# Last expert's down projection in two halves of its columns: the first half's rows put back and added before the second half is done

## The reference

```python
def swiglu(h, w_up, w_down):
    g, u = jnp.split(h @ w_up, 2, axis=-1)
    return (jax.nn.silu(g) * u) @ w_down

def moe_swiglu(h, w_router, w_up, w_down):
    logits = jnp.einsum('bld,de->ble', h, w_router, ...)
    top_v, top_i = lax.top_k(logits, TOP_K)          # TOP_K = 2
    top_w = jax.nn.softmax(top_v, axis=-1)
    combine = ...                                     # (tokens, 8), two entries per token
    out = jnp.zeros(h.shape, jnp.float32)
    for e in range(N_EXPERTS):                        # 8 experts
        out = out + combine[..., e:e + 1] * swiglu(h, w_up[e], w_down[e])
    return out.astype(h.dtype)

# x = x + moe_swiglu(rms_norm(x), ...);  y_prompt, y_sample are x after this layer
```

## Time and profile before

| | |
|---|---|
| median of 3 runs | 2094.9 us (2094.56 to 2096.92) |
| span of the profiled execution (first to last instruction) | 2093.1 us |
| PE busy | 2059.4 us (98%) |
| DVE, ACT, POOL busy | 788.0, 405.0, 157.3 us |
| DMA: bytes moved | 548.81 MB; about 410 GB/s over the experts |
| last expert's down projection, PE | 672 MATMULs, 2043.07 to 2084.1 us |
| from its end to the last instruction | 9.0 us |

### The profile page before, as it was taken

How to read it: one execution, slowest core, us unless ns; L and a number is a source line. 1 busy time by engine, 2 the same in 40 slices (tenths; PEclk the granted TensorE clock), 3 DMA queues, 4 the chain that set the end, 5 groups by cost and what they waited for, 6 DMA issues and landing times.

```text
span 2093.1 us, 45743 instructions
## 1 busy us (share of the span) xinstructions
PE 2059.4 (98%) x20245; PEld 1494.6 (71%) x20245; DVE 788.0 (38%) x1501; ACT 405.0 (19%) x772; POOL 157.3 (8%) x222
## 2 busy tenths in 40 slices
PE   7999999999999999999999999999999999999998
PEld 5977777778999997777777746565665656565645
DVE  5896333545676578643255310010101010101013
ACT  3423424312221143433341200000000000000000
POOL 3501020000000031112100010000000000000001
PEclk9999999999999999999999999999999999999999
DMA  5434535695554543453477699999999999999996
GB/s 168 142 109 142 171 115 162 190 276 155 149 154 147 159 141 122 128 161 116 151 202 229 258 364 412 408 411 409 411 409 411 408 410 410 405 415 396 412 410 241
DMA packets 287993, 548.81 MB, mean 262 GB/s; under 512 B 12883, under 2 KB 218501, under 8 KB 271348
## 3 DMA queue, kind: packets, MB, share of 16 engines
q1 hardware_dynamic: 279808, 535.85, 70.9%
q10 hardware_dynamic: 6644, 5.58, 0.9%
q0 software_dynamic: 1344, 4.45, 0.6%
HBM read 527.15 MB, written 22.50 MB: 263 GB/s over the span
## 4 chain that ended last, share of the span: by engine, by line
PE 96%; DVE 2%; POOL 1%; issue 1%; ACT 1%; POOLq 0%; DVEq 0%; ACTq 0%
PE bank L1080 93%; PE bank L1086 3%; ACT mem L2056 1%; DVE mem L2542 0%; DVE mem L2879 0%; DVE mem L2546 0%; DVE hflat L2575 0%; POOL quarterm L937 0%; DVE mem L2905 0%; POOL lmask L913 0%; POOL lmask L915 0%; DVE col L2912 0%; DVE hflat L2542 0%; DVE mem L2916 0%; DVE xT L3428 0%
## 5 line engine op out<-in xcount | busy, mean ns | idle before, releaser
L1080 PE MATMUL bank<-mem 128*32 128x256 f32 (+9 forms) x13288 | 1100.5, 387 | 11.3 <-DVE mem L2879 3.5
L1080 PEld LDWEIGHTS bank<-mem 128*32 128x32 f32 (+3 forms) x13288 | 793.8, 128 | 298.5 <-issue 47.7
L1080 PE MATMUL bank<-hflat,mem 128*128 128x288 f32 (+3 forms) x2688 | 572.8, 371 | 0.9 <-ACT hflat L2056 0.7
L1080 PEld LDWEIGHTS bank<-hflat,mem 128*128 128x128 f32 (+2 forms) x2688 | 443.3, 188 | 102.9 <-issue 12.2
L2056 ACT ACTIVATE mem<-bank 128x288 f32<-128x288 f32 (+10 forms) x423 | 180.1, 430 | 822.9 <-PE bank L1080 758.3
L1080 PE MATMUL bank<-mem,steps 128*32 128x384 f32 (+1 forms) x3072 | 290.8, 539 | 0.0
L1080 PEld LDWEIGHTS bank<-mem,steps 128*32 128x32 f32 x3072 | 148.2, 110 | 139.0 <-issue 24.7
L2542 DVE TENSOR_TENSOR mem<-mem 128x512 f32<-128x512 f32 (+10 forms) x336 | 234.6, 725 | 29.0 <-PE bank L1080 18.5
L2546 DVE SCALAR_TENSOR_TENSOR hflat<-hflat,bank 128x512 f32<-128x512 f32 x24 | 15.1, 683 | 410.8 <-ACT hflat L2056 410.8
L2056 ACT ACTIVATE hflat<-bank 128x512 f32<-128x512 f32 (+1 forms) x40 | 19.6, 554 | 567.4 <-PE bank L1080 567.4
L2056 ACT ACTIVATE mem<-mem 128x1152 f32<-128x1152 f32 (+9 forms) x125 | 92.1, 739 | 99.2 <-DVE mem L2634 63.9
(11 more groups left out here) (250 smaller groups left out, 740.4 us busy)
## 6 DMA issues: line engine op xcount, KB each, us to landing
mem<-in_w_moe_up_dram SPq DMA_DIRECT2D x64, 2048.0 KB, 20.9
mem<-in_w_moe_down_dram SPq DMA_DIRECT2D x56, 2048.0 KB, 21.3
mem<-in_w_moe_up_dram SPq DMA_DIRECT2D x32, 2304.0 KB, 22.9
mem<-in_w_in_dram SPq DMA_DIRECT2D x70, 1024.0 KB, 5.3
mem<-in_w_moe_up_dram SPq DMA_DIRECT2D x16, 1536.0 KB, 21.8
mem<-in_w_ffn_up_dram SPq DMA_DIRECT2D x44, 512.0 KB, 5.2
mem<-in_cache_kv_w_dram SPq DMA_DIRECT2D x26, 512.0 KB, 4.8
mem<-in_cache_kv_w_dram SPq DMA_DIRECT2D x74, 128.0 KB, 4.9
```

The source lines that it names most:

```text
L1080: return mm(out, lhsT, rhs, start=start, stop=stop, skip_group_check=True)
```

## The change

Only the last expert's down projection and what follows it are changed; the other experts run the same code, and their instructions keep their order.

- The 28 row blocks by 1024 columns are taken as two halves of 512 columns. Seven slabs still carry them (`last_down`): eight row blocks of half a width each, slab 17 (SHARED) with the last four of half 0 and the first four of half 1. A slab is still 2 MB, but in rows of 2048 bytes, and slab 17 comes in two DMAs.
- A product now has 128 columns in place of 256, so a slab has 96 products, which is 192 pairs of MATMUL and LDWEIGHTS. Half 0 accumulates in bank 6, half 1 in bank 7.
- ACT copies half 0 (128 x 384) when slab 17 has been used, half 1 (128 x 384) after slab 20.
- PE puts half 0 back, all three token blocks, between slab 18 and slab 19 (`rows_put_back(0, tb)`: 36 products of 128 columns, 72 pairs), into banks 0 to 3; half 1 behind slab 20, in the order of before (tb 0, tb 1, a wait for DVE's first addition of half 1, tb 2).
- DVE first waits for half 0's rows and adds them (three instructions over 512 columns), then the six additions of the gathered rows and the rank steps, then half 1 (three over 512 columns).
- SP stores six pieces of 512 columns in place of three of 1024: half 0's three when the gathered rows are in, half 1's as they are added.
- The wait for slab 17's weights counts two landings (`eslab_in`), and the counts of the semaphore `y_added` go from 9 to 12 in a round.

```diff
+        last_down = [((0, 0, 8),), ((0, 8, 8),), ((0, 16, 8),), ((0, 24, 4), (1, 0, 4)), ((1, 4, 8),), ((1, 12, 8),),
+                     ((1, 20, 8),)]
+        SHARED = 17
...
+                        if kind == "d" and e == NEXP - 1:
+                            c0 = 0
+                            for h, row, rows in last_down[n - 14]:
+                                sp.dma_start(eslot[n % MRING][:, c0:c0 + 512 * rows].rearrange("p (k n) -> p k n", k=rows),
+                                             down_v[:, e, row:row + rows, 512 * h:512 * h + 512]
+                                             ).then_inc(slab_here[n % MRING], 16)
...
+                for h in range(2):
+                    for b, (t0, n) in enumerate(BLK):
...
+                        sp.wait_ge(y_added, 12 * r + (9 if h == 0 else 10 + b))
+                        sp.dma_start(dst[:, 512 * h:512 * h + 512], xrow[b][0:n, 512 * h:512 * h + 512]
+                                     ).then_inc(out_stored, 16)
...
+                    def last_slab_down(n):
+                        pe.wait_ge(*eslab_in(r, e, n))
+                        c0 = 0
+                        for h, row, rows in last_down[n - 14]:
+                            w = eslot[n % MRING][:, c0:c0 + 512 * rows].rearrange("p (k n) -> p k n", k=rows)
+                            for i in range(rows):
+                                t = row + i
+                                for b in range(TT):
+                                    for o in range(4):
+                                        ins = put(bank[y_bank[h]][32 * o:32 * o + 32, P * b:P * b + P],
+                                                  hidT[:, b, t, :], w[:, i, P * o:P * o + P], t == 0 and b == 0, t == 27)
+                            c0 += 512 * rows
+                        ins.then_inc(*lup("m_slab"))
+
+                    def rows_put_back(h, tb):
+                        nt = BLK[tb][1]
+                        for b in range(TT):
+                            for o in range(4):
+                                rows = slice(32 * o, 32 * o + 32)
+                                acc = bank[o + (4 if h and tb == 1 else 0)][0:nt, P * tb:P * tb + P]
+                                ins = put(acc, last_cols[b][rows, BLK[tb][0]:BLK[tb][0] + nt],
+                                          yb[rows, b, P * h:P * h + P], b == 0 and (h == 1 or tb == 0), b == TT - 1)
+                        if h == 1 or tb == 2:
+                            ins.then_inc(last_rows, 1)
...
-                        if n == 17:
+                        if n == (17 if e < NEXP - 1 else 15):
                             pe.wait_ge(*lat("m_hidT", it, 2 * TT))
+                        if e == NEXP - 1 and n == SHARED + 1:
+                            pe.wait_ge(*lat("m_y", it, 1))
+                            for tb in range(3):
+                                rows_put_back(0, tb)
...
-                for tb, (t0, nt) in enumerate(BLK):
+                pe.wait_ge(y_added, 12 * r + 3)
+                pe.wait_ge(*lat("m_y", expert(r, NEXP - 1), 2))
+                for tb in range(3):
                     if tb == 2:
-                        pe.wait_ge(y_added, 9 * r + 7)
+                        pe.wait_ge(y_added, 12 * r + 10)
...
+                    rows_put_back(1, tb)
...
+                        for h in range(2):
+                            act.wait_ge(*lat("m_slab", it, done_after["d"] if h else SHARED + 1))
+                            fn(yb[:, :, P * h:P * h + P], bank[6 + h][:, 0:3 * P].rearrange("p (b n) -> p b n", b=TT),
+                               ACT.Copy).then_inc(*lup("m_y"))
...
+                def add_last(h, b):
+                    n = BLK[b][1]
+                    x = xrow[b][0:n, 512 * h:512 * h + 512].rearrange("t (o c) -> t o c", o=4)
+                    y0 = 4 if h and b == 1 else 0
+                    ve.scalar_tensor_tensor(x, banks[0:n, y0:y0 + 4, P * b:P * b + P], masked[0:n, b, 1:2], x,
+                                            ALU.mult, ALU.add).then_inc(y_added, 1)
+                dve.wait_ge(last_rows, 4 * r + 1)
+                for b in range(3):
+                    add_last(0, b)
                 dve.wait_ge(rows_back, 96 * (r + 1))
...
-                for b, (t0, n) in enumerate(BLK):
-                    dve.wait_ge(last_rows, 3 * r + b + 1)
-                    x = xrow[b][0:n, :].rearrange("t (o c) -> t o c", o=4)
...
+                for b in range(3):
+                    dve.wait_ge(last_rows, 4 * r + b + 2)
+                    add_last(1, b)
```

More of the change, by code:

```diff
@@ L700, in eslab_view, with eslab_in @@
             return eslot[n % MRING][:, 0:nk * w].rearrange("p (k n) -> p k n", k=nk)
-        def eslab_in(it, n):
-            return slab_here[n % MRING], 16 * (it * PERSLOT + n // MRING + 1)
+        def eslab_in(r, e, n):
+            count = 16 * (expert(r, e) * PERSLOT + n // MRING + 1)
+            if n % MRING == SHARED % MRING:
+                count = count + 16 * r + (16 if e == NEXP - 1 and n == SHARED else 0)
+            return slab_here[n % MRING], count
         def eslab_used(it, n):
@@ L873, in _ @@
                         load_rounds(sp, end)
-                for b, (t0, n) in enumerate(BLK):
-                    dst = y_prompt[0, t0:t0 + n, :] if t0 < TP else y_sample.rearrange("b i d -> (b i) d")
-                    sp.wait_ge(y_added, 9 * r + 7 + b)
-                    sp.dma_start(dst, xrow[b][0:n, :]).then_inc(out_stored, 16)
+                for h in range(2):
+                    for b, (t0, n) in enumerate(BLK):
+                        dst = y_prompt[0, t0:t0 + n, :] if t0 < TP else y_sample.rearrange("b i d -> (b i) d")
+                        sp.wait_ge(y_added, 12 * r + (9 if h == 0 else 10 + b))
+                        sp.dma_start(dst[:, 512 * h:512 * h + 512], xrow[b][0:n, 512 * h:512 * h + 512]
+                                     ).then_inc(out_stored, 16)
             sp.wait_ge(stored, 16 * stores[0])
@@ L1972, in slab_down @@
                         c = eslabs[n][1] // 4
-                        pe.wait_ge(*eslab_in(it, n))
+                        pe.wait_ge(*eslab_in(r, e, n))
                         w = eslab_view(n)
@@ L2012, in _ @@
                     for n in range(14, 21):
-                        slab_down(n)
-                        if n == 17:
+                        if e < NEXP - 1:
+                            slab_down(n)
+                        else:
+                            last_slab_down(n)
+                        if n == (17 if e < NEXP - 1 else 15):
                             pe.wait_ge(*lat("m_hidT", it, 2 * TT))
+                        if e == NEXP - 1 and n == SHARED + 1:
+                            pe.wait_ge(*lat("m_y", it, 1))
+                            for tb in range(3):
+                                rows_put_back(0, tb)
                     if e == 0:
                         load_rounds(pe, end)
-                for tb, (t0, nt) in enumerate(BLK):
+                pe.wait_ge(y_added, 12 * r + 3)
+                pe.sem_inc(wait_passed, 1)
+                pe.wait_ge(*lat("m_y", expert(r, NEXP - 1), 2))
+                pe.sem_inc(wait_passed, 1)
+                for tb in range(3):
                     if tb == 2:
-                        pe.wait_ge(y_added, 9 * r + 7)
+                        pe.wait_ge(y_added, 12 * r + 10)
                         pe.sem_inc(wait_passed, 1)
[L2022 to L2030, removed]
+                    rows_put_back(1, tb)
+                pe.wait_ge(y_added, 12 * r + 12)
                 pe.sem_inc(wait_passed, 1)
@@ L2512, in _ @@
                         load_rounds(act, end)
[L2513 to L2516, removed]
+                    if e == NEXP - 1:
+                        for h in range(2):
+                            act.wait_ge(*lat("m_slab", it, done_after["d"] if h else SHARED + 1))
+                            fn(yb[:, :, P * h:P * h + P], bank[6 + h][:, 0:3 * P].rearrange("p (b n) -> p b n", b=TT),
+                               ACT.Copy).then_inc(*lup("m_y"))
+                    else:
+                        act.wait_ge(*lat("m_slab", it, done_after["d"]))
+                        yf = yb.rearrange("p b n -> p (b n)")
+                        fn(yf[:, 0:512], bank[6][:, :], ACT.Copy).then_inc(*lup("m_y"))
+                        fn(yf[:, 512:768], bank[7][:, 0:256], ACT.Copy).then_inc(*lup("m_y"))
                     if e < NEXP - 1:
@@ L3411, in _ @@
                         load_rounds(dve, end)
+                def add_last(h, b):
[7 more added lines that the diff above has]
+                    add_last(0, b)
                 dve.wait_ge(rows_back, 96 * (r + 1))
                 for b in range(3):
+                    dve.wait_ge(y_added, 12 * r + b + 1)
                     add_expert(b, ylo, masked[0:BLK[b][1], b, 0:1])
                 for b in range(3):
[L3416 removed]
+                    dve.wait_ge(y_added, 12 * r + b + 4)
```

(11 more changed lines are left out.)

2 lines of the change are left out of this document (1 added, 1 removed).

## The result

The changed kernel takes 2106.44 us (median of 5 runs, 2104.69 to 2107.61) against 2094.9 us before (5 runs beside it, 2093.7 to 2098.06): ratio 1.0053, 95% interval 1.0042 to 1.0064. It is slower, by 11.5 us. The forecast was 2101.3 us, its range 2094.0 to 2106.5.

What follows compares the result with a forecast made beforehand. PE, busy for 98%, was taken as the bound. Terms -2.6 (tail), +0.5 (products), +2.2 (half 0's put back), +0.1 (DVE) gave +0.2; with 6.2 for late instructions, 2094.9 became 2101.3 us, range 2094.0 to 2106.5.

Steps and rivals of the forecast that it cites:

- PE's instructions as the term that decides: Last down projection: doubled instructions outrun their supply while DMA engines are full; 6.2 us more, chance 0.52.
- At the nearer row, 4.9 us a packet: Supply beside full DMA queues: 4.9 us per 128 pairs, from one stop at the loop's start; other end 6.8 us.
- 4.4 packets lose 1.4 us each: 6.2 us: Down products until about 2074: 4.4 late packets, each taking 4.9 us where PE needs 3.5.
- The present stops: PE's 4.5 us of stops beside POOL's gathers, kept unchanged in the forecast; growth by 2.1 us only in the range.
- Products at 0.11 us a group: Last down projection: 336 groups of four 128-column MATMULs at 0.11 us, 0.5 us more in all.
- Put back of half 0 and the tail: Half 0's put back before slab 19 adds 2.2 us on PE; the work behind slab 20 shrinks by 2.6 us.
- now it is even: DVE free just when half 1's first put back needs it, before 2.7 us early; 0.1 us, bounds 0 and 0.6.
- Weights in short rows hide: Last expert's slabs in 2048-byte rows take 5.5 us for 5.1; hidden, without cover 2.8 us at most.
- 1: Rival: instruction supply is no limit; 2095.1 us, or 2097.2 with grown stops; chance 0.28.
- 4: Rival: slabs come late by 2.8 us, with supply no limit; 2097.9 us; chance 0.04.
- 2: Rival: the present stops are one late packet and go away; 2090.6 us; chance 0.08.
- Rival 3: PE's clock drops behind the forecast's stops, 3.5 us more, 2104.8 us; chance 0.08 on top of the supply limit.

Runs made afterwards that it cites:

- Experiment 1: Kernel before, each down product of the last expert cut into two of 128 columns, same slabs, order and put back: 2107.92 us against 2094.42.
- experiment 2: Kernel before, last expert's down slabs each loaded by two transfers of 2048-byte rows, products still of 256 columns: 2095.31 us against 2094.42.
- experiment 3: Changed kernel, each transfer of the last expert's down weights bringing one row block in place of eight or four: 2099.22 us against 2094.42 for the kernel before.
- experiment 6: Changed kernel, PE's put back of half 0 moved from between slabs 18 and 19 to behind slab 20: 2116.57 us against 2095.42 for the kernel before.
- experiment 5: Changed kernel, POOL's six gathers issued two at a time after slabs 15, 16 and 17: 2104.97 us against 2095.42 for the kernel before.
- experiments 4: Kernel before, POOL's six gathers issued two each after slabs 14, 15 and 16 in place of all after slab 15: 2093.11 us against 2094.42.
- experiment 7: Kernel before, POOL's six gathers issued two each after slabs 15, 16 and 17: 2092.46 us against 2095.42.

## Why the prediction was right in its kind and short in its size

- *The bound, and PE's instructions as the term that decides.* Right: slower, by stops "issue" at every 128th pair while the DMA engines are full, and none after. Experiment 1 shows that the doubled instructions do it, experiment 2 that the rows don't, experiment 3 that full queues are needed.
- *"At the nearer row, 4.9 us a packet".* This is the step that failed. Between full queues a packet took 6.21 and 6.29 us (2049.95 to 2056.16 to 2062.45), near the other end of my bounds, 6.8. The earlier trace rows measured a first late packet, not one of a series: by the packets' times in the trace it began 2.6 us after PE's first product of the 128, where in the changed kernel's series it is 3.8 us. The DMA queues' rows of the changed kernel show the packet in flight for only a small part of that period:
```profile
q1 hardware_dynamic: 943, 1.90, 105.2%
...
q8 instruction: 1, 0.02, 5.0%
```
  The first is of the window 2055.0 to 2059.9: no instructions come in while PE works off the packet it has. The other is of 2059.9 to 2061.3: the next one is fetched, beside the weights' 2048-byte packets, and PE goes on at 2062.45. So a packet isn't fetched over the whole period, and dividing a bandwidth wouldn't have given the number. The period is three pieces: 3.8 us from PE's first product of a packet to the start of the next packet, 1.1 us in flight, 1.3 us until PE goes on (2056.16, 2060.01, 2061.14, 2062.45).
- *"4.4 packets lose 1.4 us each: 6.2 us".* Five boundaries lost 9.5 us: 0.89, 2.65, 2.73, 2.20 and 1.01, each the time from start to start of the timeline's rows less 27.8 ns for each MATMUL (10.69 us / 384; 128 of them for the row of 127). That is 3.3 us over the forecast's 6.2, most of its miss of 4.3 us in the stops. The rest is in pauses at boundaries while the DMA engines are idle, 1.2 us in all: 0.4 before half 0 is put back and 0.8 in the last 384 MATMULs, most of it in pauses of about 0.3 us that are too short for a row of their own.
- *The present stops, "which I keep as they are".* Nearly so here: 3.9 us beside the gathers after, 4.3 before, since two of the six gathers ran while PE stood for a packet anyway. That is chance of timing and no rule. The growth kept for the range, 2.1 us, is there in other traces of the halved products: the same stretch cost 5.0 us in experiment 1, 5.9 in experiment 3 and 5.8 in experiment 6, whose PE runs the same products as the changed kernel up to there.
- *Products at 0.11 us a group.* 0.111 in experiment 5's trace; 0.119 in the changed kernel's last 96 groups, with the pauses just named. Without stops the cut costs 0.4 us, for 0.5: right.
- *Put back of half 0 and the tail.* 2.3 and -2.4 us, for 2.2 and -2.6: right.
- *DVE "now it is even".* It was free 0.8 us early. Its timeline: the first new addition, the last rank step, the first addition of half 1.
```profile
2087.91 1.41 DVE L3470 SCALAR_TENSOR_TENSOR xT<-bank,mem,xT 128x512 f32<-128x512 f32 x2 [39.85 <-PE bank L1096]
...
2099.95 0.17 DVE L3363 SCALAR_TENSOR_TENSOR mem<-mem 128x3 int32<-128x3 f32 x1
...
2100.93 1.42 DVE L3470 SCALAR_TENSOR_TENSOR xT<-bank,mem,xT 128x512 f32<-128x512 f32 x2 [0.81 <-PE bank L1096]
```
- *Weights in short rows hide.* Right (experiment 2).
- *Rivals.* 1 and 4 fell with the stops, 2 with the stretch beside the gathers, which experiment 3 shows to be no late packet. Rival 3, the clock, wasn't in the changed kernel's trace (1.00 in all its stops) but in those of experiments 1, 3, 5 and 6: 0.50 to 0.61 for 3 to 4 us behind a stop or a slow stretch, worth 1.3 to 1.7 us of PE's time, and 0 to 0.5 us where a late packet follows.
- *The chances* don't quite follow from their terms: these add up to 0.51 slower, 0.45 same and 0.04 faster, for 0.52, 0.42 and 0.06.
- *"Mostly hidden"*, as the Trainium skill ("Runtime: NRT & Kernel Launch", section "Instruction fetch mechanics") calls the cost of crossing a block of 256 instructions: it agrees with experiment 3 ahead of the gathers, where the DMA share was 0.09, and with products of 256 columns beside full queues. It doesn't agree with products of 128 columns beside full queues, where a block cost 2.7 us.
- *The sum.* -2.4 + 0.4 + 2.3 + 10.5 = 10.8 us in the trace, 11.5 us between the medians, against 6.4. The median ends 0.06 us inside the range's upper end, and two of the five runs lie outside: that the range held is luck. Its upper end was put together from late packets of 9.6 us and grown stops, of which this trace has the first alone.

## What to carry to other kernels

Count instructions as well as columns: where PE's pairs come faster than one packet of 256 instructions in about 6.3 us, 49 ns a pair, and the DMA queues are full of weights, halving the columns of a product makes PE stand for its instructions, here for some 10 us against 2.4 saved behind the end. A finer grain belongs where the DMA engines are idle: here slabs 19 and 20, which ran 384 MATMULs of 128 columns with 0.8 us of short pauses. (No run cut these two alone.) And an idle stretch with the releaser "issue" beside POOL's indirect transfers could be removed by issuing these in pairs, so late that they don't come in ahead of a slab that PE needs (experiments 4 and 7, products of 256 columns).

## What the runs showed of the hardware

- The period of PE's packets beside full DMA queues was 6.2 to 6.8 us in four kernels (the changed one, experiments 1, 5 and 6), also where a lower clock made PE's share of it 5.3 or 5.4 in place of 3.7 us.
- In these series a packet began 3.8 to 3.9 us after PE's first product of the packet before it in eleven of twelve cases (4.5 in the other), at the full and at the lower clock; it was in flight for 1.0 to 1.1 us, and PE went on 1.3 to 1.5 us after it had landed.
- A series of POOL's indirect transfers, six in 7 to 8 us, slows PE's instructions to six pairs every 0.73 us, also where the DMA engines were nearly idle before them (experiment 3). Pairs of them, 3 us apart, do nothing to products of 256 columns (experiment 7); products of 128 columns still came six every 0.76 us beside the second pair in experiment 5. It isn't a late packet of instructions (experiment 3). Through what they act isn't settled: no run changed the number or the size of the transfers alone.
- Why the next packet begins no sooner than 3.8 us after PE has gone on, and what PE waits for in the 1.3 us after it has landed, stays open too.
